# The second norm's scale row in one burst ahead of the attention heads, and thinner late rotations

## The reference

```
def modulation(cvec, w_mod_l, b_mod_l):
    m = jax.nn.silu(cvec) @ w_mod_l + b_mod_l
    return m.reshape(cvec.shape[0], 6, D_MODEL)

def trunk_layer(x, mod, ...):
    sh1, sc1, g1, sh2, sc2, g2 = [mod[:, i][:, None, :] for i in range(6)]
    h = rms_norm(x, n1) * (1.0 + sc1) + sh1
    proj = h @ w_in
    q, k, v, u = jnp.split(proj, [Q_W, Q_W + KV_W, Q_W + 2 * KV_W], axis=-1)
    q, k = rms_norm(q, qg), rms_norm(k, kg)      # per head; rotary on latent rows
    attn = block_attention(q, k_all, v_all)      # 8 heads of 64
    conv = conv_module(u, dw_w, dw_b, ln_g, ln_b)   # 31 taps, 512 channels, layer norm
    x = x + g1 * (jnp.concatenate([attn, conv], axis=-1) @ w_out)
    h2 = rms_norm(x, n2) * (1.0 + sc2) + sh2
    x = x + g2 * grouped_moe(h2, ...)            # 16 experts, top 2
    return x, k, v
```

## Time and profile before

| what | us |
|---|---|
| timed runs | 1114.33, 1105.78, 1114.35 (median 1114.33) |
| profiled execution | 1104.32 |
| its span, first to last instruction | 1102.5 |
| TensorE, VectorE busy | 952.6 (86%), 403.2 (37%) |
| ScalarE, GpSimd busy | 163.2 (15%), 124.3 (11%) |

### The profile page before, as it was taken

One profiled execution on the slowest core, in us unless ns is written; L12 is line 12 of the kernel. 1 busy time (PEld: TensorE's weight loads), 2 busy tenths in 40 slices (PEclk: granted clock), 3 DMA queues, 4 the chain that ended last, 5 costly groups with the idle time before them and its releaser, 6 DMA issues. The chain is left out here.

```text
span 1102.5 us, 12356 instructions
## 1 busy us (share of the span) xinstructions
PE 952.6 (86%) x4764; PEld 449.7 (41%) x4764; DVE 403.2 (37%) x896; ACT 163.2 (15%) x370; POOL 124.3 (11%) x188
## 2 busy tenths in 40 slices
PE   3699899997898989978689969999778988988886
PEld 2355445464333333333246544545523333333332
DVE  0199754146211110111346995533531111110117
ACT  2101334120000000000140014421000000000001
POOL 1002201511000010000221021060210000000010
PEclk9799899987998999989889998999679998999999
DMA  9929964368999996999970475225966999999942
GB/s 339 384 111 341 320 263 150 90 245 348 424 419 427 424 389 265 419 425 424 361 266 24 152 267 234 77 94 179 369 259 245 411 425 428 421 423 425 421 158 77
DMA packets 64570, 328.59 MB, mean 298 GB/s; under 512 B 7448, under 2 KB 10184, under 8 KB 48084
## 3 DMA queue, kind: packets, MB, share of 16 engines
q1 hardware_dynamic: 44224, 277.89, 62.7%
q0 software_dynamic: 9072, 27.89, 6.9%
q10 hardware_dynamic: 11172, 21.42, 5.9%
HBM read 305.88 MB, written 21.30 MB: 297 GB/s over the span
## 5 line engine op out<-in xcount | busy, mean ns | idle before, releaser
L1779 PE MATMUL ps<-big 128*64 128x512 f32 x1024 | 239.7, 623 | 36.7 <-DMA big<-in_w_up_dram 17.6
L1795 PE MATMUL ps<-big,scr 128*64 128x512 f32 x624 | 147.9, 615 | 9.2 <-DVE scr L1426 3.7
L1475 PE MATMUL ps<-big 128*128 128x384 f32 (+2 forms) x448 | 148.3, 493 | 5.1 <-ACT big L786 5.1
L1779 PEld LDWEIGHTS ps<-big 128*64 128x64 f32 x1024 | 79.1, 143 | 173.3 <-issue 161.6
L1122 DVE SCALAR_TENSOR_TENSOR scr<-scr,convw 128x384 f32<-128x384 f32 x240 | 134.1, 611 | 2.3
L1439 DVE TENSOR_TENSOR scr<-ps,scr 128x256 f32<-128x256 f32 x32 | 13.6, 425 | 274.1 <-ACT scr L962 274.0
L1475 PEld LDWEIGHTS ps<-big 128*128 128x128 f32 x448 | 86.0, 193 | 65.1 <-issue 29.9
L1795 PEld LDWEIGHTS ps<-big,scr 128*64 128x64 f32 x624 | 48.6, 141 | 95.7 <-issue 92.5
L1695 PE MATMUL ps<-big 128*128 128x512 f32 x192 | 84.4, 594 | 1.4 <-ACT big L835 1.4
L962 ACT ACTIVATE scr<-ps 128x256 f32<-128x256 f32 x32 | 12.3, 384 | 320.4 <-PE ps L1779 320.4
L1779 PE MATMUL ps<-big,scr 128*64 128x512 f32 x224 | 51.3, 612 | 5.9 <-DVE scr L1415 5.9
(11 more groups left out here) (231 smaller groups left out, 819.8 us busy)
## 6 DMA issues: line engine op xcount, KB each, us to landing
big<-in_w_gate_dram SPq DMA_DIRECT2D x32, 2048.0 KB, 18.9
big<-in_w_up_dram SPq DMA_DIRECT2D x32, 2048.0 KB, 24.0
big<-in_w_down_dram SPq DMA_DIRECT2D x32, 2048.0 KB, 21.1
big<-in_w_mod_dram SPq DMA_DIRECT2D x23, 2048.0 KB, 14.9
big<-in_w_in_dram SPq DMA_DIRECT2D x6, 2048.0 KB, 27.7
expert_rows<-scr ACTq DMA_DIRECT2D x68, 128.0 KB, 8.4
big<-in_w_out_dram SPq DMA_DIRECT2D x4, 2048.0 KB, 20.3
expert_rows<-x ACTq DMA_DIRECT2D x1, 7168.0 KB, 42.3
```

The source lines that it names most:

```text
L1475: mm = pe.matmul(out, stationary(k), moving(k), start=(k == 0), stop=(k == n - 1))
L1779: mm = pe.matmul(ps[b * TT:(b + 1) * TT, bank, :].rearrange("p (m n) -> p m n", m=2), tokens(k), w[:, :, k, b * HF:(b + 1) * HF], start=(k ...
L1795: mm = pe.matmul(ps[b * TT:(b + 1) * TT, bank, :], src[:, k % 2 * P + k // 2 * TT:k % 2 * P + (k // 2 + 1) * TT], w[:, k, b * SEG:(b + 1) ...
```

## The change

Vector 4 no longer goes through `head_fill`, which is removed with its half-vectors. It is computed by `vector(l, 4)` on four column groups like the others: in layer 0 all eight row blocks behind head 0's scores; in layer 1 (`VEC4_AHEAD`) four of them ahead of the last rotated tile's transposes, the other four behind head 0's scores. VectorE takes it right after head 0's maxima, as one row of 256 columns on all partitions. Its bias now comes together with that of vector 3 (`rowBS`), and so do the stores of the two. The norm gain is laid out on the lanes, in four loads of 32 partitions, at the same place of GpSimd's list. The late rotations keep two taps instead of six (tile 2 in layer 0, tiles 1 and 2 in layer 1); what is left goes into the heads, five a head as before.

```
-TAKES = [0, 1, 2, 3, 8, 9, 5]
+TAKES = [0, 1, 2, 3, 4, 5]
-EARLY_TAPS, ROPE_TAPS, BETWEEN_TAPS, LATE_TAPS, HEAD_TAPS = 80, 6, 0, 0, 5
+EARLY_TAPS, HEAD_TAPS = 80, 5
+ROPE_TAPS = [[6, 6, 2], [6, 2, 2]]
-HEAD_FILL = [(8 + hd // 4, hd % 4 * (KD // 4), (hd % 4 + 1) * (KD // 4)) for hd in range(HEADS)]
+VEC4_AHEAD = [0, 4]
...
-                lane_in(pool, rowB, b_mod[l:l + 1, 3 * D:4 * D], rowB_in)
-                pool.dma_start(rowS, b_mod[l:l + 1, 4 * D:5 * D].broadcast_to([2, D])).then_inc(rowB_in, 16)
+                lane_in(pool, rowBS, b_mod[l:l + 1, 3 * D:5 * D], rowB_in)
...
                 pool.wait_ge(slot_used[slot_of(("in", l, 3))], uses(("in", l, 3)))
-                pool.dma_start(gainB, norm2_g[l:l + 1, :].broadcast_to([2, D])).then_inc(gain_in, 16)
+                lane_in(pool, gainB, norm2_g[l:l + 1, :], gain_in)
 
                 pool.wait_ge(mod_done, l + 1)
-                lane_out(pool, mod_dram[:, 3 * D:4 * D], rowB, modB_st)
-                pool.dma_start(mod_dram[:, 4 * D:5 * D], rowS).then_inc(modB_st, 16)
+                lane_out(pool, mod_dram[:, 3 * D:5 * D], rowBS, modB_st)
...
+                row = (rowC, rowB, rowS, rowG)[c - 2]
+                v.tensor_tensor(row, ps[:, bank, 0:LW], row, ALU.add).then_inc(mod_taken, 1)
+                if c == 4:
+                    dve.wait_ge(gain_in, (l + 1) * LANES * 16)
                     dve.wait_ge(mod_taken, taken_at(l, c))
-                    ins = v.scalar_tensor_tensor(row, row, 1.0, gain, ALU.add, ALU.mult)
-                    if c != 8:
-                        ins.then_inc(mod_done, 1)
+                    v.scalar_tensor_tensor(row, row, 1.0, gainB, ALU.add, ALU.mult).then_inc(mod_done, 1)
...
                 score_max(0)
+                mod_take(l, 4)
                 for hd in range(HEADS):
                     if 0 < hd < HEADS - 1:
                         score_max(hd + 1)
                     taps(min(HEAD_TAPS, len(CONV_ORDER) - conv_at))
                     if hd == 0:
                         score_max(1)
-                    if HEAD_FILL[hd][2] == KD:
-                        mod_take(l, HEAD_FILL[hd][0])
                     head_output(hd)
...
                 for t in range(TILES):
+                    if t == 2 and VEC4_AHEAD[l]:
+                        vector(l, 4, 0, VEC4_AHEAD[l])
                     pe.wait_ge(rope_ready, l * 3 + t + 1)
...
                     scores(0, t)
+                vector(l, 4, VEC4_AHEAD[l], KD)
                 for hd in range(HEADS):
...
+                        if hd == 0 and t == 2:
+                            pe.wait_ge(mod_taken, taken_at(l, 4))
...
-                    head_fill(l, hd)
```

More of the change, by code:

```diff
@@ L184, in mod_bank @@
         return 1
-    return {3: 0, 8: 0, 9: 0, 5: 3}[j]
+    return {3: 0, 4: 3, 5: 3}[j]
 def col_bank(l, s):
@@ L996, in mod_take @@
                 if c == 3:
-                    dve.wait_ge(rowB_in, (l + 1) * (LANES + 1) * 16)
+                    dve.wait_ge(rowB_in, (l + 1) * LANES * 16)
                 if c == 5:
                     dve.wait_ge(rowG_in, (l + 1) * LANES * 16)
[L1000 to L1004, removed]
+                n = pieces(l, c)[-1][0]
+                dve.wait_ge(slot_used[slot_of(n)], uses(n))
                 if c < 2:
@@ L1140, in rope @@
                     if t or l == 0:
-                        taps(ROPE_TAPS)
+                        taps(ROPE_TAPS[l][t])
                     dve.wait_ge(qk_rstd, l * 3 + t + 1)
@@ L1185, in _ @@
                     rope(0)
-                    taps(BETWEEN_TAPS)
                 else:
-                    taps(BETWEEN_TAPS + ROPE_TAPS)
+                    taps(ROPE_TAPS[l][0])
                 rope(1)
@@ L1191, in _ @@
                 mod_take(l, 2)
-                taps(LATE_TAPS)
                 mod_take(l, 3)
@@ L1494, in vector @@
                             mm.then_inc(slot_used[slot_of(n)], 1)
-            def head_fill(l, hd):
-                c, k0, k1 = HEAD_FILL[hd]
-                if k0 == 0:
-                    pe.wait_ge(mod_taken, taken_at(l, 3 if c == 8 else 8))
-                for n, a, b in pieces(l, 4):
-                    for k in range(max(a, k0), min(b, k1)):
-                        if c == 8 and k == a:
-                            loaded(n)
-                        mm = pe.matmul(ps[0:2, mod_bank(l, c), :], cs_rep[:, k, 0:2],
-                                       slot_k(slot_of(n), b - a)[:, k - a, (c - 8) * SEG:(c - 7) * SEG],
-                                       start=(k == 0), stop=(k == KD - 1))
-                        if c == 8 and k == KD - 1:
-                            mm.then_inc(mod_half_ps, 1)
-                        if c == 9 and k == b - 1:
-                            mm.then_inc(slot_used[slot_of(n)], 1)
             def columns(l, s_):
```

10 lines of the change are left out of this document (5 added, 5 removed).

## The result

| kernel | device us, median (lowest to highest) | profiled execution | its span | its granted clock |
|---|---|---|---|---|
| before | 1114.34 (1105.78 to 1117.77) | 1104.32 | 1102.5 | 0.933 |
| changed | 1158.90 (1151.30 to 1159.76) | 1159.15 | 1157.3 | 0.872 |

The change makes the kernel 4.0% slower: the ratio is 1.0401, with a 95% interval of 1.0352 to 1.0450. Forecast were 1102 us, 1.1% faster, in a range of 1087 to 1113.

A forecast was written before the change was run, and what follows sets the result against it. TensorE's instruction list was taken to bound the heads; gains less the gain wait and clock left 7.4 us in layer 0 and 4.6 in layer 1, together 12 off the 1114.3 median: 1102.3 us, range 1087 to 1113.

The forecast's parts named there:

- What bounds it, heads 1 to 6: Attention heads 1 to 6: TensorE's list without filler takes 4.87 us a head, not 6.68; 10.2 and 10.5 us gained.
- the lag of 0.7 and 0.4 us charged for chained taps: Heads 1 to 6: the last 16 taps depend on each other, so VectorE lags; 0.7 us in layer 0, 0.4 in layer 1.
- Head 7 and the chain behind the heads: Last head gains 1.8 us in layer 0, 0 in layer 1; GpSimd's layer-norm chain starts 1.1 us earlier in each.
- The new wait: VectorE waits for the norm gain before head 0's taps; head 1 starts 4.0 us later in layer 0, 5.3 in layer 1.
- rival A: Before head 0's taps: the gain does not wait for the gateB broadcast; 3.3 us more, a saving of 15; chance 0.13.
- rival B: Before head 0's taps: the gain's landing takes longer, leaving a saving of 1 or 15 us slower; chance 0.12 with anything slower.
- the 0.2 that the prediction added for them: Before head 0's taps: issuing four gain loads instead of one delays the landing by an estimated 0.2 us.
- The burst: Vector 4's row blocks behind head 0's scores: at most 7.2 us, hidden under the wait for the gain, so no cost.
- The clock: Head 1 starts at half speed after TensorE idles; costs 1.7 us per layer, ends 0 and 3.4.
- Rival C: Attention heads: half clock for 7 to 10 us per layer, or chained taps; saving only 4 to 8 us; chance 0.19.

The follow-up runs named there:

- filled waits, early gain: Changed kernel with the norm gain's loads issued ahead of vector 2's stores and broadcast, and unused products in TensorE's waits ahead of the heads: 1076.45 us, ratio 0.9691.
- the wait filled in part and in full: Changed kernel, late gain, unused products ahead of the heads and behind head 0: seven and nine there gave 1120.99 to 1149.23 us, ten and fifteen 1098.16.
- the early gain: Changed kernel with the norm gain's four loads issued ahead of vector 2's stores and broadcast; run twice: 1080.63 to 1118.88 us, then 1084.25 to 1117.88.
- the wait alone: Kernel before, filler kept, with VectorE waiting for the norm gain behind head 0's row maxima: 1131.32 us, ratio 1.0140.

## Why the prediction was wrong

**What bounds it, heads 1 to 6: right at full clock.** The forecast was 4.87 us a head and 10.2 and 10.5 us a layer. With the clock held it is 29.20 and 29.24 us for six heads instead of 40.08, 10.9 a layer; the lag of 0.7 and 0.4 us charged for chained taps doesn't show.

**Head 7 and the chain behind the heads: right.** In layer 1, at full clock (filled waits, early gain), head 7's products wait 1.14 us for head 6's output where 1.8 was forecast. GpSimd takes up the layer norm 0.2 us after the statistics are ready, not 1.1. VectorE's and GpSimd's timelines of the changed kernel, layer 1:

```profile
768.68 0.18 DVE L1202 BATCH_NORM_AGGREGATE stat<-stat 128x2 f32<-128x6 f32 x1
...
769.05 0.18 POOL L549 TENSOR_SCALAR stat<-stat 128x1 f32<-128x1 f32 x1 [61.08 <-DVE stat L1202]
```

**The new wait: right in kind, a little small.** The wait is there, on VectorE, for the gain's DMA, before head 0's taps, and the gain lands 1.1 and 1.6 us behind the broadcast, not ahead of it, so rival A is out. From L1009 to head 1's transposes it is 3.8 us (146.61 to 150.43), forecast 4.0. From the last rotation's transposes to head 1 it is 150.43 - 127.77 = 22.7 us in layer 0, against 147.3 - 126.8 = 20.5 forecast, and 708.87 - 684.79 = 24.1 in layer 1, against 681.5 - 659.2 = 22.3. So the landing took some 2 us a layer longer than set, under the 3 that were to show rival B and far from its price. The broadcast itself took 10.4 and 11.4 us instead of 8.9 and 9.8, and the issue of the four loads took 2.00 us (L318 above) where one took 0.52; the 0.2 that the prediction added for them was an estimate that no run shows. The burst cost nothing beside the wait, as forecast; with the gain early and the waits filled it is on the path: in layer 1 TensorE goes from the scores to head 0 without a gap, and in layer 0 a gap of 1.39 us is left, in which the burst waits for its weights.

**The clock: the step that failed.** "Half speed over 3.2 us loses 1.6; I take 1.7 per layer. The ends are 0 and [...] 3.4." It loses some 56 us, 28 in each layer. Rival C had the clock "at half for 7 to 10 us per layer", at a cost of "2 to 4 us more in each layer"; its sign, a head over 5.5 us, came, at 8.93, but for the whole stage. What failed is the reading of the earlier trace rows: I took the 3.2 and 6.8 us as the time that a fall lasts, whatever TensorE does. But the second of them ended in head 0's filler, as did the same stretch in layer 0. TensorE's timeline of the kernel before, layer 1:

```profile
671.79 2.92 PE L1505 MATMUL ps<-big,cs_rep 128*2 128x512 f32 x4
```

The change takes the filler out of the same heads into which it puts the wait. With the wait and the filler the clock was back 9 us after head 1 began in layer 1 and 21 us after in layer 0; with the wait and without the filler it stayed down to the end of the heads; with neither, executions differed. The right price is that of the stage: seven heads at 8.93 instead of 4.87 us are 28 us a layer (head 0 stands ahead of the gain's wait).

With the clock held and all else as the change has it, the kernel is at 1098.16, 10.9 us under the 1109.02 beside it; the sum without its clock term was 12 + 2 x 1.7 = 15.4, and the landings' 2 us a layer are about the difference. The profiles have the 10.9 in the two attention stages: 62.1 and 69.6 us (as above) against 68.3 and 74.5 in the kernel before.

The Trainium skill, "TensorE: Matmul & The Clock Gate", section "What's actually happening", says that the throttled clock is the default and that activity releases it. The trace agrees with the first half, the clock at 0.50 in the wait of 6.41 us, and with the second only in part: TensorE's records fill 53.57 of 53.57 us and the clock is at 0.50 all along (busy time in the records is modelled, so it may hold gaps that don't show). Its section "HAM oscillation — how this bites in real kernels" says that a wait between groups of products can throttle TensorE and that the next group then starts slow; the pair with the wait filled in part and in full agrees, 0.50 behind 5.46 us and 1.00 behind 0.19.

**What stays open.** Why the clock came back ahead of head 0 in one execution of the early gain and not in another, behind the same wait and with the same instructions. In the slower profile it fell inside the wait, at 647.3, in the faster one at 650.1, 0.9 us behind its end. Nor is it shown what in TensorE's work brings it back: it came back in pairs of 512-column products, in the 256-column burst (early gain, 657.0) and in the transposes behind the heads, but not in the heads without a filler, and in layer 0 of the wait alone not behind the first pair. Nor does a profile show which layer was at half in the executions that were only timed.

## What to carry to other kernels

Filler work is worth what it does to the clock, too: before it is taken out, look whether it is the work in which the clock comes back behind the stage's waits, and price the stage at half clock for its whole length, not for the length of the last fall. When a change makes a time split into levels a fixed step apart, look at the granted clock by stage in one profile of each level. A wait of TensorE ahead of a long stage of short products may be worth filling with products that nobody reads: here seven of them, in time that was lost anyway, made 1115 or 1081 into a steady 1076.

## What the runs showed of the hardware

- Half clock that lasts as long as a stage: 54.93 us at 0.50 in layer 1 of the changed kernel with TensorE busy throughout (708.87 to 763.80), and on to 771.2, in the transposes behind the heads.
- The same instruction list at 1081 and at 1117 us, and three levels of 1097, 1130 and 1163.
- One 512-column product a head left the clock at 0.50 for 53.63 us; with two it was at 1.00 right behind the first pair (676.70). In the kernel before with the wait alone, the same fall ended in the first pair in layer 1 and in the second in layer 0.
- The gain's four loads, 32 KB each, were there 13.0 us after the issue of the broadcast ahead of them on GpSimd's queue in layer 1, where the one load of 8 KB had been there after 0.74 + 9.4 = 10.1.
